# Attention items in another order: prompt items first, the last items' values inside the output projection, modulation weights issued ahead of the exchange

## The reference

```
kv = (all_ckv @ p['w_ukv']).reshape(b, lk, MLA_HEADS, QK_NOPE + V_HEAD)
s = jnp.einsum('bqhd,bkhd->bhqk', qi, k).astype(jnp.float32) * scale
p = jax.nn.softmax(s, axis=-1).astype(v.dtype)
return jnp.einsum('bhqk,bkhd->bqhd', p, v)
...
out = jnp.concatenate([attn_out, conv_out, cmlp_out], axis=-1) @ p['w_out']
x = x + g1 * mix
mod_lat = (jax.nn.silu(c) @ w_ada[l] + b_ada[l])[:, None, :]
```

## Time and profile before

| | us |
|---|---|
| median of three runs | 2457.82 (2455.4 to 2459.53) |
| profiled execution, its own time | 2462.69 |
| its span in the trace | 2460.9 |
| TensorE busy | 2323.0 (94%) |
| VectorE busy | 748.9 (30%) |
| ScalarE busy | 510.8 (21%) |
| attention loop and its end, layer 0 | 323.4 to 594.8 |
| the same, layer 1 | 1531.4 to 1803.8 |

### The profile page before, as it was taken

The page is one execution under the profiler, slowest core; times in us unless marked ns, Lnnn a source line. Parts: engine busy times, 40 slices in busy tenths (PEclk is TensorE's granted clock), DMA queues, the critical chain, the costliest instruction groups (busy, mean ns, idle before and its releaser), DMA issues.

```text
span 2460.9 us, 30238 instructions
## 1 busy us (share of the span) xinstructions
PE 2323.0 (94%) x12252; PEld 1522.1 (62%) x12252; DVE 748.9 (30%) x1413; ACT 510.8 (21%) x1046; POOL 279.0 (11%) x438
## 2 busy tenths in 40 slices
PE   6999998998997999999999999899989969999996
PEld 4545545655445887888755455456644458887885
DVE  2401244553237111111142022455523551111113
ACT  3310122222334101010142102222223320101003
POOL 2000010201001112111210000310100011112111
PEclk8999999999998999999999999999999969999998
DMA  9100259775546888888940002785732268888888
GB/s 332 34 7 15 71 117 231 189 162 114 198 146 225 263 276 270 275 276 291 328 154 17 22 0 86 168 191 112 124 102 103 86 218 275 278 275 275 274 280 300
DMA packets 216024, 440.70 MB, mean 179 GB/s; under 512 B 32032, under 2 KB 75224, under 8 KB 215936
## 3 DMA queue, kind: packets, MB, share of 16 engines
q1 hardware_dynamic: 167920, 358.71, 46.0%
q0 software_dynamic: 22928, 54.56, 9.1%
q10 hardware_dynamic: 25088, 26.23, 5.3%
HBM read 339.34 MB, written 47.65 MB: 157 GB/s over the span
## 4 chain that ended last, share of the span: by engine, by line
PE 84%; DMA 5%; DVE 4%; SPq 3%; ACTq 1%; ACT 1%; issue 1%; DVEq 0%; POOLq 0%
PE PS L1367 11%; PE PS L1374 11%; PE PS L1206 11%; PE PS L1399 9%; PE PS L992 8%; PE PS L946 6%; PE PS L1085 5%; PE PS L933 5%; PE PS L1142 4%; PE PS L1097 3%; PE PS L1393 2%; DMA r<-in_b_ada_dram 2%; PE PS L1046 1%; ACTq L1598 1%; SPq L528 1%; PE PS L1352 1%
## 5 line engine op out<-in xcount | busy, mean ns | idle before, releaser
L1367 PEld LDWEIGHTS PS<-r,ring 128*128 128x128 f32 x2048 | 282.6, 191 | 15.6 <-issue 15.6
L1206 PE MATMUL PS<-ring,mix 128*128 128x512 f32 x640 | 290.5, 601 | 0.0
L1367 PE MATMUL PS<-r,ring 128*128 128x160 f32 x2048 | 284.7, 300 | 0.5 <-ACT r L1697 0.4
L1374 PE MATMUL PS<-r,ring 128*128 128x160 f32 x2048 | 283.4, 299 | 0.0
L1374 PEld LDWEIGHTS PS<-r,ring 128*128 128x128 f32 x2048 | 279.9, 190 | 0.0
L1399 PE MATMUL PS<-ring,r 128*128 128x512 f32 x496 | 221.1, 599 | 0.0
L992 PE MATMUL PS<-r,ring 128*128 128x512 f32 (+1 forms) x576 | 208.4, 521 | 1.6 <-ACT r L1491 1.6
L1206 PEld LDWEIGHTS PS<-ring,mix 128*128 128x128 f32 x640 | 117.6, 192 | 128.5 <-issue 128.0
L1085 PE MATMUL PS<-lat,r 128*128 128x512 f32 (+1 forms) x416 | 190.2, 592 | 3.8 <-ACT r L1534 2.7
L2170 DVE TENSOR_TENSOR r<-r,PS 128x320 f32<-128x320 f32 x64 | 31.2, 488 | 498.8 <-PE PS L1374 498.8
L1142 PE MATMUL PS<-r 128*128 128x256 f32 x768 | 175.8, 387 | 5.2 <-DMA r<-r 3.2
(11 more groups left out here) (306 smaller groups left out, 2191.5 us busy)
## 6 DMA issues: line engine op xcount, KB each, us to landing
ring<-in_w_gate_dram SPq DMA_DIRECT2D x32, 2048.0 KB, 10.1
ring<-in_w_up_dram SPq DMA_DIRECT2D x32, 2048.0 KB, 11.7
ring<-in_w_down_dram SPq DMA_DIRECT2D x31, 2048.0 KB, 9.3
ring<-in_w_ada_dram SPq DMA_DIRECT2D x15, 2048.0 KB, 9.6
r<-r SPq DMA_DIRECT2D x128, 96.0 KB
r<-r ACTq DMA_DIRECT2D x128, 96.0 KB
r<-ring ACTq DMA_DIRECT2D x128, 96.0 KB
r<-ring SPq DMA_DIRECT2D x128, 96.0 KB
```

The lines of the kernel that those rows point to most:

```text
L1206: ins = pe.matmul(psum(2 * (s % 2) + n, 512), mix[:, k, tile * P:(tile + 1) * P], W_OUT[n][:, k, :], start=(k == 0), stop=(k == KD - 1))
L1367: ins = pe.matmul(PS[:, b // 2, (b % 2) * 256:(b % 2) * 256 + SLOTS], W_G[:, k, b * P:(b + 1) * P], XST[par][:, k, :], start=(k == 0), sto ...
L1374: ins = pe.matmul(PS[:, 2 + b // 2, (b % 2) * 256:(b % 2) * 256 + SLOTS], W_U[:, k, b * P:(b + 1) * P], XST[par][:, k, :], start=(k == 0), ...
```

## The change

Four things change. (1) `ITEMS` begins with the two prompt items. (2) The values of items 16 and 17, the last two, which are now sample tiles, leave the end of the loop: they stand inside the projection, behind the first column half of tile 0 and behind the routing of tile 0 in tile 1. Item 17 gets a target buffer (`PTL`, in the space of the queries) and a PSUM bank of its own, and its whole exchange is issued by SP. (3) The value heads are cut anew into ten chunks: six of 512 tokens and two of the prompt (two heads each) ahead of the projection, and two of 512 tokens inside tile 2. The projection of a tile takes the other mixers' rows first, the heads' rows last. (4) SP issues the weights of block n + 2 ahead of exchange n, as soon as block n is computed; the bias rows stay behind the exchange.

```diff
-ITEMS = []
+ITEMS = [(_p, PROMPT_TILES) for _p in range(2)]
 for _p in range(2):
     ITEMS += [(_p, t) for t in range(PT, NT)]
-ITEMS += [(_p, PROMPT_TILES) for _p in range(2)]
...
+UV_CHUNKS = [(0, NP, 6), (1, NP, 0), (2, NP, 1), (3, NP, 2), (0, NP + 512, 3), (1, NP + 512, 4), (0, 0, 5), (2, 0, 6),
+             (2, NP + 512, 4), (3, NP + 512, 5)]
+NU = len(UV_CHUNKS)
+UV_ON_ACT = [0, 1, 2, 3, 4, 5, 8]
...
+        def values_of(n):
+            return PS[:, 4, 0:256] if n == NI - 1 else PS[:, 7, 0:256]
+        def turned(n):
+            return PTL if n == NI - 1 else PTr[n % 2]
...
+                def load_ada_weights(i):
...
+                    if i >= 2:
+                        sp.wait_ge(ada_summed, 1 + ADA_AT[l] + i - 1)
+                    sp.dma_start(ada_w[i % 2], ada_src[la, n]).then_inc(ada_landed[i % 2], 16)
+                def load_ada_bias(i):
...
                     if i >= 2:
                         sp.wait_ge(ada_biased, 1 + ADA_AT[l] + i - 1)
-                    sp.dma_start(ada_w[i % 2], ada_src[la, n]).then_inc(ada_landed[i % 2], 16)
                     for j in range(4):
...
                 for n in range(NI):
-                    exchange(n, (0, 1))
-                    if n + 2 < len(ADA_ITEMS[l]):
-                        load_ada(n + 2)
+                    load_ada_weights(n + 2)
+                    exchange(n, (0, 1) if n < NI - 1 else range(4))
+                    load_ada_bias(n + 2)
...
                 n = NI - 1
-                pe.wait_ge(o_divided, at(l, NI, 8))
+                times_values(n - 2, range(12))
+                pe.wait_ge(ada_copied, ADA_AT[l] + len(ADA_ITEMS[l]))
                 value_heads(0)
-                value_heads(1)
                 pe.wait_ge(exp_done, at(l, 2 * NI, 2 * n + 1))
-                value_heads(2)
-                value_heads(3)
-                times_values(n - 1, range(12))
+                pe.wait_ge(o_divided, at(l, NI, 14))
+                for m in (1, 2, 3):
+                    value_heads(m)
                 pe.wait_ge(exp_done, at(l, 2 * NI, 2 * n + 2))
...
+                for m in (4, 5, 6):
+                    value_heads(m)
+                value_head_copied(0)
                 value_heads(7)
-                times_values(n, range(12))
...
                 for s in range(NT):
-                    if s == 1:
-                        pe.wait_ge(o_divided, at(l, NI, NI))
-                        prompt_value_heads(0)
-                        prompt_value_heads(1)
                     project(s, 0, 0)
                     turn_sums(s - 1)
                     project(s, 0, 1)
                     if s == 0:
+                        times_values(NI - 2, range(12))
+                        value_head_copied(7)
...
                     route(s - 1)
+                    if s == 1:
+                        times_values(NI - 1, range(12))
+                    if s == 2:
+                        pe.wait_ge(o_divided, at(l, NI, NI))
+                        value_heads(8)
+                        value_heads(9)
                     project(s, 1, 0)
...
```

More of the change, by code:

```diff
@@ L60, in groups_of, with uvh_count @@
     return (4, 64) if ITEMS[n][1] is PROMPT_TILES else (2, 384)
-UV_CHUNKS = [(NP, 0, 2), (NP, 1, 5), (NP + 512, 0, 0), (NP + 512, 1, 1), (NP, 2, 3), (NP, 3, 4), (NP + 512, 2, 2), (NP + 512, 3, 5)]
-NU = len(UV_CHUNKS) + 2
+UV_CHUNKS = [(0, NP, 6), (1, NP, 0), (2, NP, 1), (3, NP, 2), (0, NP + 512, 3), (1, NP + 512, 4), (0, 0, 5), (2, 0, 6),
+             (2, NP + 512, 4), (3, NP + 512, 5)]
+NU = len(UV_CHUNKS)
+UV_ON_ACT = [0, 1, 2, 3, 4, 5, 8]
+def uvh_count(m):
+    return (0, UV_ON_ACT.index(m) + 1) if m in UV_ON_ACT else (1, m + 1 - sum(1 for u in UV_ON_ACT if u < m))
 OUT_ORDER = list(range(PT, NT)) + list(range(PT))
@@ L529, in exchange @@
                                 .then_inc(pt_landed[n % 2], 16)
[L531 to L532 removed]
+                for i in range(2):
+                    load_ada_weights(i)
+                    load_ada_bias(i)
                 for n in range(NI):
[L534 to L536 removed]
+                    load_ada_weights(n + 2)
+                    exchange(n, (0, 1) if n < NI - 1 else range(4))
+                    load_ada_bias(n + 2)
                     if n == len(ADA_ITEMS[l]):
@@ L1201, in project @@
                         if s == 0:
-                            for i in range(2):
-                                pe.wait_ge(uvh_copied[i], at(l, NU // 2, NU // 2 - 1))
+                            value_head_copied(2)
+                        if s == 1:
+                            value_head_copied(4)
+                    if s == 0 and n == 0 and half == 1:
+                        value_head_copied(3)
                     tile = OUT_ORDER[s]
-                    for k in range(4 * half, 4 * half + 4):
+                    for k in range(4 - 4 * half, 8 - 4 * half):
                         ins = pe.matmul(psum(2 * (s % 2) + n, 512), mix[:, k, tile * P:(tile + 1) * P], W_OUT[n][:, k, :],
-                                        start=(k == 0), stop=(k == KD - 1))
+                                        start=(k == 4), stop=(k == 3))
                     if half == 1:
@@ L1215, in turn_sums @@
                     if t == 0:
-                        for i in range(2):
-                            pe.wait_ge(uvh_copied[i], at(l, NU // 2, NU // 2))
+                        value_head_copied(5)
+                        value_head_copied(6)
+                    if t == 1:
+                        pe.wait_ge(o_copied, at(l, NI, NI))
+                    if t == 2:
+                        value_head_copied(8)
+                        value_head_copied(9)
                     if t >= 1:
@@ L1604, in _ @@
                     copy_out(n - 2)
-                    exchange(n, (2, 3))
-                copy_value_heads(0)
-                copy_value_heads(2)
+                    if n < NI - 1:
+                        exchange(n, (2, 3))
+                for m in range(6):
+                    copy_value_heads(m)
                 copy_out(NI - 2)
-                copy_value_heads(4)
-                copy_value_heads(6)
-                copy_out(NI - 1)
                 act.wait_ge(mod_ready, 2 * l + 2)
```

90 lines of the change are left out of this document (46 added, 44 removed).

## The result

The changed kernel takes 2446.94 us (median of six runs, 2442.2 to 2456.23), the kernel before 2460.79 (six runs, 2455.4 to 2467.73): 0.9946 of the time, 95% interval [0.9922, 0.9969], 13.9 us won where 15.1 were forecast. The profiled execution of the changed kernel took 2456.23 us, the slowest of its six, so the pair of profiles shows only 6.5 us. Layer 1's loop starts at 1550.18 where it started at 1531.44: in this pair layer 0 lost 18.7 us and layer 1 won 25.2.

A forecast was written before the change was run, and what follows sets the result against it. TensorE holds 84% of the chain of waits, so only its idle or slow time can be won. The terms 26.4 + 4 + 2 - 17.3 = 15.1 us give 2457.82 - 15.1 = 2442.7 us, range 2426 to 2457.

The forecast's parts named there:

- the wait at tile 2: Sign: in layer 0's projection TensorE waits 12 to 17 us ahead of the third tile's transposes, none in layer 1.
- the waits at the end: Sign: no TensorE wait over 1 us between the last scores and tile 1 of the projection.
- The last block of layer 0: Sign: layer 0's last modulation block comes 100 to 113 us behind the attention loop's start.
- The loop's end: End of both attention loops: waits for exchanges and slow running go, 9.95 us in layer 0, 16.44 in layer 1; 26.4 won.
- The late loads ahead of XD: Layer 0's projection, third tile: late weight loads hold back XD; 14.4 us wait plus 2.85 slow running, 17.3 us lost.
- The loop's start in layer 0: Attention loop up to the last modulation block, prompt items first: less waiting, a gain of 4 us.
- rival Three: Loop's start: exchanges landing later than 31 us after their scores hold blocks and next weights in a loop; 2480 us, chance 0.07.
- The loop's start in layer 1: Attention loop up to the last modulation block, prompt items first: less waiting, a gain of 2 us.
- The output weights: Wait of 3.15 us with 2.97 slow running in layer 1; may vanish or appear in layer 0, 6 us either way.
- One: Rival, layer 0's projection: XD's load slips between the late weights and is not held back; 2425.4 us, chance 0.12.
- Two: Rival, loop's start: prompt exchanges cost by their bytes, 2.7 us instead of 8; 2426.7 us, chance 0.08.
- Four: Rival, loop's end: it still waits, item 16's exchange being 9 us late in each layer; 2461 us, chance 0.10.

The follow-up runs named there:

- experiment 3: Changed kernel with the values of items 16 and 17 put back ahead of the projection: 2467.29 us, ratio 1.0008.
- experiment 1: Changed kernel with layer 0's three late weight loads issued one by one behind the XD loads of tiles 3, 4 and 5: 2431.81 us, ratio 0.9899.
- experiment 2: Kernel before, with layer 0's three late weight loads also waiting for the routing of tile 1: 2475.67 us, ratio 1.0064.
- experiment 5: Kernel of experiment 1 with prompt exchanges in 1024-byte pieces instead of 256, blocks landing in wrong places: 2438.66 us, ratio 0.991.
- experiment 7's second kernel: Kernel before, with the inverses of the row sums transposed on VectorE and stored in 128-byte instead of four-byte pieces: 2418.9 us, ratio 0.9829.
- experiment 7: Kernel of experiment 1 with the inverses transposed on VectorE and stored in 128-byte instead of four-byte pieces: 2407.61 us, ratio 0.9785.
- experiment 6: Kernel of experiment 1 with modulation blocks spaced at items 0, 1, 3, 5 and on, output weights behind them: 2444.17 us, ratio 0.992.
- experiment 9: Kernel of experiment 7 plus the old four-byte store, into an unread buffer, for the first 14 items of a layer: 2431.99 us, ratio 0.9884.
- experiment 8: Kernel of experiment 1 with both the block spacing of experiment 6 and the longer inverse pieces of experiment 7: 2413.05 us, ratio 0.9807.
- experiment 10: Changed kernel, late weight loads left early, with only the inverses transposed and stored in 128-byte pieces: 2423.79 us, ratio 0.9851.

## Why the prediction was right, and where not

**The number** came out as forecast, 13.9 us for 15.1, but in part by luck. The two large terms were right in mechanism and size; the start of layer 0's loop was out by 11.6 us, and the terms read from the profiled pair add up to 2.6 us only (below). The split by layers was missed: 3 us lost and 18 won were forecast, the pair has 18.7 and 25.2.

Of the signs that the prediction named, the wait at tile 2 came and the waits at the end went. The last block of layer 0 came 116.5 us behind the start and not 100 to 113, and blocks stood 27.5 us (360.40 to 387.92) and 21.4 us (403.41 to 424.80) apart, where 18 or more was to show the prediction wrong: for the loop's start it was.

**The loop's end**, +26.4: right in mechanism and size. All the waits are gone in both layers, and experiment 3 brings waits back of 19.3 us. The margins counted for items 16 and 17 held.

**The late loads ahead of XD**, -17.3: right; 15.4 measured. The wait was 13.30 for 14.4, since the sum was ready 23.8 us behind the count and not 24.9, and the slow running 2.1 for 2.85. Experiments 1 and 2 show the cause from both sides.

**The loop's start in layer 0**, +4: mis-sized, -7.6 measured. Two steps failed. I read 75 GB/s at a share of 1.01 as the price of 256-byte pieces in the prompt's exchange; experiment 5 refutes it. GpSimd's store of 512 four-byte pieces held in that very window of the kernel before:

```profile
568.70 0.76 POOL L718 DMA_DIRECT2D inv_dram<-oinv  x1 [0.49 <-DVE oinv L1935]
579.71 0.54 POOL L724 DMA_DIRECT2D lat<-inv_dram  x1 [10.25 <-DMA inv_dram<-oinv]
```

In experiment 7's second kernel the first of the same two exchanges, in the same pieces, moved 92 GB/s at a share of 0.45 (557 to 562), which is 204 at a full share. The Trainium skill (DMA: Bandwidth & Descriptors, "Why small descriptors are slow (HBM only)"), against which I set the row, says that small pieces within SBUF bear no such penalty; these two runs agree with it for 256 bytes. Then I let SyncE's half of an exchange land within 31 us of its scores. It did not: item 2's scores end at 345.7, and its half, issued from 351.61 behind 2 MB of weights, released the values at 381.12, 35.4 us later. The four-byte stores turned that order into a wait, since experiment 7 has the same order and no wait. That is rival Three's condition, once or twice in a loop and not in each of its turns.

**The loop's start in layer 1**, +2: 2.1 in this pair.

**The output weights**, kept out of the sum at 6 us either way: it went both ways, 5.95 + 2.02 lost in layer 0 and 5.1 won in layer 1, -2.9 together.

These terms make 26.4 - 15.4 - 7.6 + 2.1 - 2.9 = 2.6 us; the profiled pair shows 6.5 and the medians 13.9. The 3.9 us between sum and pair are not traced to a row. Between pair and medians lie 7.4 us, because the changed kernel's profiled execution is 9.3 us above its median and the one before 1.9. Which waits were shorter in the median run no trace shows. The 8 us at layer 0's output weights may belong to this execution: the same values wait 2.58 us in experiment 5 and not at all in experiments 1 and 3. With four-byte pieces six runs of a kernel spread over 9 to 15 us (changed kernel, experiments 1, 6 and 9), with longer pieces over 4 to 7 (experiments 7, 8 and 10).

**The rivals.** One fell: the late weights do hold XD back. Two was right in its premise, the price by bytes, and wrong in its time, because the four-byte stores and not the exchange filled the engines. Four fell with the brackets at the end.

## What to carry to other kernels

A DMA share of 1 says that the engines are occupied, not that bytes set the pace (here a full share carried 214 GB/s with the four-byte stores and 269 without); put GB/s beside it, and where full engines move little, look for a transfer of few bytes in many pieces, whatever queue it is in. Here it showed as a late landing of others, and the waits of TensorE named those; its own engine's waits named it (12 us for a kilobyte). And of a count that releases DMAs, follow what stands behind these in the queue: moving the last of its events moved a load of x by as much.

## What the runs showed of the hardware

A store of 256 four-byte pieces (1 KB) landed 12.2 us after its issue (median of five at the start of layer 0's loop; 9.2 over that loop) in the changed kernel; turned into 128-byte pieces, GpSimd's waits for the stores fell from 326 us over the execution to 138. These rows are the waits of GpSimd, first the changed kernel's, then experiment 7's (total, times, longest):

```profile
POOL lat L751 <- DMA inv_dram<-oinv: 326.2, 35, 13.1
```

```profile
POOL lat L751 <- DMA inv_dram<-oinv_t: 137.6, 34, 7.8
```

The Trainium skill (DMA: Bandwidth & Descriptors, "Rules for kernel authors") says that a non-contiguous last dimension becomes one descriptor per element and should be rearranged. That rearranging pays the runs show, 44 us in the kernel before; the descriptors by themselves no trace shows. The Trainium skill (DMA: Bandwidth & Descriptors, "Specifications") puts the size for full rate at 512 bytes or more; 128 bytes, below it, were enough here to end the waits, with a thirty-second of the pieces.

The granted clock stood at 0.50, the lower of its two levels (1.2 GHz), in the window 376 to 380 above, after TensorE had been idle since 370.8; the first values behind that wait took 6.87 us for 5.34. So each long wait costs a second time, 1.5 to 3 us in the rows of values shown.
